# Peer experts: fetches and sums of the 64 gathered tokens spread over the gate groups, shorter tails, and two tensors moved in SBUF

## The chip, the cores and the metric

The program runs on one core of a Trainium2 chip. Its time is the device time of one execution in microseconds (us). The kernel before took 3847.72 us (median of three runs, 3847.21 to 3849.86). The engines are PE (TensorE, with its weight loads shown as PEld), DVE (VectorE), ACT (ScalarE), POOL (GpSimd) and SP (SyncE, here only a queue that starts DMAs).

## The reference

A first block (a two-branch recurrent mixer, then PEER experts) and a second block (attention, MLP, state-space mixer, MLP) act on 512 tokens of width 1024. The change touches mainly the PEER layer. Cut to what matters:

```python
def peer(h, wq, k1, k2, u, v):            # 8 heads, top 16 of 128 x 128 experts per head
    q = (tok @ wq).reshape(-1, 8, 2, 128)
    s1, s2 = q[:, :, 0] @ k1.T, q[:, :, 1] @ k2.T     # 128 scores each, per head
    v1, i1 = top_k(s1, 16); v2, i2 = top_k(s2, 16)
    top_s, top_c = top_k((v1[..., :, None] + v2[..., None, :]).reshape(..., 256), 16)
    expert = i1[top_c // 16] * 128 + i2[top_c % 16]
    gate = softmax(top_s)
    act = gelu(einsum("pd,ped->pe", x, u[expert]))    # 128 experts of a token
    return einsum("pe,ped->pd", gate * act, v[expert])
```

The MLP of the second block is `(relu(h @ w1 + b1) ** 2) @ w2 + b2` with 4096 hidden units.

## The kernel before

Everything is computed with features on the 128 partitions and tokens along the free axis. A float32 product is made of three matmuls of rounded parts (`parts_product`, line 1330): high times high, high times low, low times high. So a weight tile of 128 x 1024 costs 24 matmuls. Its high part is written by ACT (`high`), its low part (raw minus high) by POOL in the first part of the PEER layer (line 1595), by DVE elsewhere.

**Two ways for two groups of tokens.** 448 of the 512 tokens are computed densely: all 16,384 experts' activations for all of them (128 tiles of `u`, the `up(n)` of the code, each 24 matmuls of 448 columns), then a dense matrix of gates, then 128 tiles of `v`. The other 64 tokens (FEW) are computed from gathered rows: two experts' rows for the 64 tokens fill 128 partitions, so 64 calls (CALLS) fetch all rows of `u`, and 64 calls all rows of `v`. `fetch_up` and `fetch_down` are these indirect DMAs, issued by POOL; `few_dots` multiplies a fetched row of `u` with the token and sums it, `few_add` adds a fetched row of `v`, weighted, to a sum in PSUM (line 1953, DVE).

**The gates.** For the dense tokens a gate matrix per token is the product of two one-hot matrices. DVE writes them for eight tokens at a time (`one_hot`: line 2011 one instruction, line 2015 eight), PE multiplies (`gate`, line 1700, 16 records), ACT copies the result from PSUM to the tensor `slab` (line 1806). There are four quarters of the tokens (`TT`), each with 14 such groups. When a quarter is complete, ACT starts four DMAs that write the slab (7.3 MB) to HBM (line 1853). The slab is single: ACT's first copy of the next quarter waits for all four.

**The order.** It is written out by hand, the same in the program of each engine. 48 tiles of `u` go with the eight heads, 7 more (AHEAD) follow while DVE finishes the last top-16. Then for each quarter: 14 gate groups, with one tile of `u` behind those groups for which `between(g)` holds (the last group among them), then a *tail* of TAILS tiles without gates, during which the slab goes out. Tile n uses place p = n + 16 in the stream of weight tiles. POOL's loop runs over the places: it writes the low part of place p, and then issues the fetches that belong to that place. All that stands on POOL is served in order. `fetch_down(c)` waits until the sum number c - 4 is done, since its row's buffer is one of four (OWN), and all later low parts wait behind it. `few_add(c)` on DVE waits for its row to land, and the one-hots of the next quarter stand behind the sums.

Before the change the first four fetches of a quarter are issued two places ahead of its tail, the other twelve by twos at the first six places of the tail (all 16 sums stand behind group 13 on DVE). After the last quarter the `v` tiles begin: each needs an activation tile and a gate tile read back from HBM (`load_pair`, SP), multiplied on DVE (`weigh`).

**Places in SBUF.** Tensors are laid out one behind the other. In the first MLP the moving operand `h_parts` begins where the scan's tables begin, and `w_parts` lies behind the tables, 43,584 bytes per partition further. In the second MLP that distance is 32,768 bytes. In the mixer's output stage `merged_hi` lies at the place of `h`, 118,336 bytes ahead of `w_parts`. The tensor `lb` (64 bytes per partition) lay behind `ident`.

## Time and profile before

| | |
|---|---|
| median of 3 runs | 3847.72 us |
| the profiled execution: its own time, and the span from first to last instruction | 3844.51 us, 3842.7 us |
| PE busy | 3597.3 us, 94% of the span |
| DVE, ACT, POOL busy | 63%, 42%, 33% |
| mean granted TensorE clock | 0.972 |
| the gate section, first gate to first `v` tile | 1446.49 to 1974.32 us: 527.83 us |

PE is the engine to look at. Its idle stretches and the slices in which its clock is granted at half are what a change can win; what the other engines do matters where PE waits for them. In the section below a timeline row has start, duration, engine and line, operation, output<-inputs, shape, number of instructions, and in brackets the idle time before it and what ended it. Ends of matmuls are modelled, so neighbours overlap by some 0.2 us.

### The profile page before, as it was taken

The numbers are of one execution on the slowest core, as the hardware profiler recorded it, in microseconds if no ns is written. First come the engines' busy times: TensorE is split into PE (matmuls) and PEld (weight loads), VectorE is DVE, ScalarE is ACT, GpSimd is POOL, SyncE is SP. The second block draws the span as 40 slices with busy tenths as digits, with TensorE's granted clock in tenths as the row PEclk, the third lists the DMA queues.
The fourth block names the chain that finished last, engine by engine and source line by source line (L and its number), as shares of the span: only waits on it lengthen the run. The fifth ranks groups of instructions, "written<-read, shape, count | busy, mean of one in ns | idle before, by whom it ended". The sixth has DMA issues, their size and how long they took to land. (4 is left out here: it accounts for less than half of the span.)

```text
span 3842.7 us, 47185 instructions
## 1 busy us (share of the span) xinstructions
PE 3597.3 (94%) x18068; PEld 3100.8 (81%) x18068; DVE 2428.3 (63%) x3743; ACT 1622.2 (42%) x2246; POOL 1248.9 (33%) x774
## 2 busy tenths in 40 slices
PE   7999989979999999888999999998999998799998
PEld 6888767768788888878889999996778887677886
DVE  6655534445379988656758878876565475856354
ACT  5555454445242234334434444445542224434222
POOL 1222122137047665354354444441020004402002
PEclk9999989989999999999999999999999999999999
DMA  5111021046247665576498889881123322132331
GB/s 183 55 50 50 17 63 50 23 138 204 103 138 235 222 232 205 204 269 244 154 364 282 285 282 284 285 260 58 42 77 105 98 90 72 29 100 82 99 95 64
DMA packets 245132, 566.26 MB, mean 147 GB/s; under 512 B 91648, under 2 KB 133904, under 8 KB 242736
## 3 DMA queue, kind: packets, MB, share of 16 engines
q1 hardware_dynamic: 203968, 396.31, 31.7%
q0 software_dynamic: 37440, 135.32, 10.5%
q10 hardware_dynamic: 3504, 31.65, 2.1%
q8 instruction: 144, 2.36, 0.2%
q14 instruction: 76, 0.62, 0.1%
HBM read 497.36 MB, written 60.82 MB: 145 GB/s over the span
## 5 line engine op out<-in xcount | busy, mean ns | idle before, releaser
L1330 PE MATMUL peer_banks<-peer_h_parts,peer_w_parts 128*128 128x448 f32 (+1 forms) x3456 | 741.6, 374 | 47.2 <-POOL peer_w_parts L1595 41.4
L1330 PEld LDWEIGHTS peer_banks<-peer_h_parts,peer_w_parts 128*128 128x128 f32 x3456 | 654.0, 191 | 117.4 <-POOL peer_w_parts L1595 51.1
L1330 PE MATMUL peer_banks<-peer_act_parts,peer_w_parts 128*128 128x448 f32 x3072 | 624.3, 365 | 0.0
L1330 PEld LDWEIGHTS peer_banks<-peer_act_parts,peer_w_parts 128*128 128x128 f32 x3072 | 576.3, 188 | 45.4
L1595 POOL TENSOR_TENSOR peer_w_parts<-slots,peer_w_parts 128x1024 fp32r<-128x1024 f32 x142 | 351.5, 2476 | 348.6 <-ACT peer_w_parts L1777 347.0
L1330 PE MATMUL ffn_ps<-h_parts,ffn_w_parts 128*128 128x512 f32 x1920 | 447.5, 395 | 18.0 <-DVE h_parts L2650 11.2
L1330 PEld LDWEIGHTS ffn_ps<-h_parts,ffn_w_parts 128*128 128x128 f32 x1920 | 362.9, 189 | 101.1 <-DVE ffn_w_parts L2488 15.8
L1330 PE MATMUL ffn_ps<-ffn_hidden,ffn_w_parts 128*128 128x512 f32 x1920 | 438.2, 390 | 1.5 <-DVE ffn_hidden L2557 1.5
L1777 ACT ACTIVATE peer_w_parts<-slots 128x1024 fp32r<-128x1024 f32 x272 | 287.1, 1055 | 322.6 <-PE peer_banks L1330 318.6
L1330 PEld LDWEIGHTS ffn_ps<-ffn_hidden,ffn_w_parts 128*128 128x128 f32 x1920 | 360.3, 188 | 77.8 <-issue 3.1
L175 POOL TENSOR_TENSOR peer_slab<-peer_slab 128x1024 f32<-128x1024 f32 x96 | 237.0, 2469 | 258.7 <-ACT peer_slab L182 258.3
L2334 ACT ACTIVATE ffn_w_parts<-slots 128x1024 fp32r<-128x1024 f32 x160 | 168.5, 1056 | 313.1 <-PE ffn_ps L1330 305.5
L2488 DVE TENSOR_TENSOR ffn_w_parts<-slots,ffn_w_parts 128x1024 fp32r<-128x1024 f32 x160 | 197.8, 1240 | 144.2 <-ACT ffn_w_parts L2334 143.8
L2038 DVE TENSOR_TENSOR peer_slab<-peer_slab 128x448 f32<-128x448 f32 x128 | 281.0, 2195 | 7.7 <-DMA peer_slab<-peer_gates 7.7
L1330 PE MATMUL hgrn_proj_ps<-h_parts,hgrn_w_parts 128*128 128x512 f32 x960 | 269.4, 413 | 8.7 <-DVE hgrn_w_parts L986 8.2
L1791 ACT ACTIVATE h<-peer_banks 128x448 f32<-128x448 f32 x128 | 69.7, 544 | 470.0 <-PE peer_banks L1330 434.7
L2048 DVE TENSOR_TENSOR peer_w_parts<-slots,peer_w_parts 128x1024 fp32r<-128x1024 f32 x128 | 157.8, 1233 | 118.5 <-ACT peer_w_parts L1777 118.4
L496 POOL TENSOR_TENSOR hgrn_w_parts<-x,hgrn_w_parts 128x1024 fp32r<-128x1024 f32 x38 | 96.2, 2531 | 342.9 <-ACT hgrn_w_parts L707 342.9
L2301 POOL TENSOR_TENSOR ffn_total<-x 128x512 f32<-128x512 f32 x4 | 5.5, 1379 | 613.9 <-DVE x L2504 613.9
L1330 PEld LDWEIGHTS hgrn_proj_ps<-h_parts,hgrn_w_parts 128*128 128x128 f32 x960 | 168.3, 190 | 39.5 <-DVE hgrn_w_parts L986 8.2
L1330 PE MATMUL gla_proj_ps<-h_parts,gla_w_parts 128*128 128x512 f32 (+1 forms) x600 | 175.7, 432 | 19.8 <-DVE gla_w_parts L1000 14.6
L1953 DVE SCALAR_TENSOR_TENSOR peer_banks<-peer_few_rows,peer_few_w,peer_banks 128x1024 f32<-128x1024 f32 x63 | 81.2, 1288 | 145.8 <-DMA peer_few_rows<-in_peer_v,peer_few_idx 141.3
(579 smaller groups left out, 5773.4 us busy)
## 6 DMA issues: line engine op xcount, KB each, us to landing
slots<-in_peer_u SPq DMA_DIRECT2D x128, 512.0 KB
slots<-in_peer_v SPq DMA_DIRECT2D x128, 512.0 KB
slots<-in_mlp_w SPq DMA_DIRECT2D x128, 512.0 KB, 3.5
peer_slab<-in_w_mod POOLq DMA_DIRECT2D x96, 512.0 KB, 4.5
peer_acts<-h SPq DMA_DIRECT2D x128, 224.0 KB
peer_gates<-peer_slab ACTq DMA_DIRECT2D x16, 1792.0 KB, 14.7
peer_slab<-peer_acts SPq DMA_DIRECT2D x128, 224.0 KB, 5.0
peer_slab<-peer_gates SPq DMA_DIRECT2D x128, 224.0 KB, 5.3
```

The lines of the kernel that those rows point to most:

```text
L175: ins = V_.tensor_tensor(self.prod[:, u, :], self.ring[:, slot, :], self.rows[:, u, :], ALU.mult)
L496: nc.gpsimd.tensor_tensor(wp[:, m % 2, 1, :], ring[m % R], wp[:, m % 2, 0, :].bitcast(F32), ALU.subtract).then_inc(w_lo, 1)
L1330: last = nc.tensor.matmul(out, w(a, k), x(b, k), start=start and k == ks[0] and n == 0, stop=stop and k == ks[-1] and n == 2)
L1595: nc.gpsimd.tensor_tensor(wp[:, p % 2, 1, :], ring.raw[:, p % R, :], wp[:, p % 2, 0, :].bitcast(F32), ALU.subtract).then_inc(w_lo, 1)
L1777: A(wp[:, p % 2, 0, :], ring.raw[:, p % R, :], ACT.Copy).then_inc(w_hi, 1)
L1791: A(stage[:, n % 4, :], a_ps[:, n % 2 * T:n % 2 * T + DENSE], ACT.Gelu).then_inc(gelu_done, 1)
L1953: V.scalar_tensor_tensor(out=few_ps, in0=few_slot(CALLS + c), scalar=w, in1=few_ps, op0=ALU.mult, op1=ALU.add).then_inc(few_added, 1)
L2038: V.tensor_tensor(wact[:, n % 2, :], act_in_sb[:, n % 4, :], gate_in_sb[:, n % 4].rearrange("p b t -> p (b t)"), ALU.mult).then_inc(weight ...
L2048: V.tensor_tensor(wp[:, p % 2, 1, :], ring.raw[:, p % R, :], wp[:, p % 2, 0, :].bitcast(F32), ALU.subtract).then_inc(v_lo, 1)
L2301: st.then(G.tensor_tensor(total[:], K.x[:, 0, :], K.x[:, 1, :], ALU.add))
L2334: A(wp[:, m % 4, 0, :], raw[:, m % R, :], ACT.Copy).then_inc(w_hi, 1)
L2488: V.tensor_tensor(wp[:, m % 4, 1, :], raw[:, m % R, :], wp[:, m % 4, 0, :].bitcast(F32), ALU.subtract).then_inc(w_lo, 1)
```

## The change

In the gate section: eight tiles of `u` move from the tails into the gate groups (a tile now stands behind every group except number 5 and 12), and the tails become 6, 6, 6 and 7 tiles. The sums of fetched `v` rows no longer all stand behind group 13: 3 of the first quarter and 11 of each later quarter follow a group's one-hot each, the tails keep 8, 8, 8 and 4. The fetches get places of their own, each two places behind the place at which the sum that frees its buffer is expected. The last eight fetches of `u` rows are issued by twos at four places, where they were issued by fours at two; their products and the weights stand earlier among the groups. Number and kind of all instructions stay the same.

In SBUF: `lb` moves ahead of `h`, so `h` and all that lies up to `ident`, and `merged_hi` with it, move up by 64 bytes. In the first MLP and the scan behind it a gap of 112 numbers (448 bytes) stands ahead of `w_parts`.

```diff
-        TAILS = (8, 8, 8, 9)
+        TAILS = (6, 6, 6, 7)
         def between(g):
-            return g % 7 in (0, 1, 3, 4, 6)
+            return g % 7 != 5
+        ADD_AFTER = [(11, 12, 13)] + [tuple(range(2, 13))] * 3
+        TAIL_ADDS = (8, 8, 8, 4)
+        def fetch_places():
+            gate_tiles = sum(between(g) for g in range(groups))
+            added = []
+            for tt in range(TT):
+                first = QU + AHEAD + sum(TAILS[:tt]) + tt * gate_tiles
+                added += [first + sum(between(x) for x in range(g)) for g in ADD_AFTER[tt]]
+                added += [first + gate_tiles + m * TAILS[tt] // TAIL_ADDS[tt] for m in range(TAIL_ADDS[tt])]
+            return [78 + c if c < OWN else min(max(82, added[c - OWN] + 2), FRONT - 1) for c in range(CALLS)]
+        places = fetch_places()
...
-                if p == 70:
-                    for c in range(7 * 8, 7 * 8 + OWN):
-                        fetch_up(c)
-                if p == 75:
-                    for c in range(7 * 8 + OWN, CALLS):
-                        fetch_up(c)
+                if p in (69, 70, 73, 74):
+                    c = 7 * 8 + 2 * (69, 70, 73, 74).index(p)
+                    fetch_up(c)
+                    fetch_up(c + 1)
...
-                    if p == tail - 2:
-                        for c in range(16 * tt, 16 * tt + OWN):
-                            fetch_down(c)
-                    if 1 <= p - tail < 7:
-                        c = 16 * tt + OWN + 2 * (p - tail - 1)
+                for c in range(CALLS):
+                    if places[c] == p:
                         fetch_down(c)
-                        fetch_down(c + 1)
...
-                    if tt == 0 and g == 9:
+                    if tt == 0 and g == 7:
                         act.wait_ge(few_dotted, CALLS)
...
-                    if tt == 0 and g == 3:
+                    if tt == 0 and g == 1:
                         few_dots(range(7 * 8, 7 * 8 + OWN))
-                    if tt == 0 and g == 8:
+                    if tt == 0 and g == 6:
                         few_dots(range(7 * 8 + OWN, CALLS))
-                    if tt == 0 and g == 11:
+                    if tt == 0 and g == 10:
                         few_weights()
-                few_add(range(16 * tt, 16 * tt + 16))
+                    if g in ADD_AFTER[tt]:
+                        few_add((c,))
+                        c += 1
+                few_add(range(c, c + TAIL_ADDS[tt]))
+                c += TAIL_ADDS[tt]
...
             keep(alias, "x_alias", [P, KT, T])
+            keep(alias, "lb_alias", [P, 16])
             merged_hi = keep(alias, "merged_hi", [P, KT, T], F32R)
         K.x = keep(ctx, "x", [P, KT, T])
+        K.lb = keep(ctx, "lb", [P, 16])
         K.h = keep(ctx, "h", [P, KT, T])
...
-        K.lb = keep(ctx, "lb", [P, 16])
...
             S = ssm_table_memory(nc, tables)
+            keep(tables, "parts_gap", [P, 112])
             ffn(nc, K, d, 0, hp, S=S)
```

POOL before, from the last fetches of the first quarter's tail to the middle of the second's. L1595 is the low part of a weight tile, L1590 a fetch of `v` rows:

```order
L1595 TENSOR_TENSOR peer_w_parts<-slots,peer_w_parts 128x1024 x10
L1590 DMA peer_few_rows<-in_peer_v,peer_few_idx 128x1024 x4
L1595 TENSOR_TENSOR peer_w_parts<-slots,peer_w_parts 128x1024 x3
L1590 DMA peer_few_rows<-in_peer_v,peer_few_idx 128x1024 x2
L1595 TENSOR_TENSOR peer_w_parts<-slots,peer_w_parts 128x1024
L1590 DMA peer_few_rows<-in_peer_v,peer_few_idx 128x1024 x2
L1595 TENSOR_TENSOR peer_w_parts<-slots,peer_w_parts 128x1024
```

POOL after, the second quarter's last gate groups and the first places of its tail (low parts are L1610, fetches L1605):

```order
L1605 DMA peer_few_rows<-in_peer_v,peer_few_idx 128x1024
L1610 TENSOR_TENSOR peer_w_parts<-slots,peer_w_parts 128x1024
L1605 DMA peer_few_rows<-in_peer_v,peer_few_idx 128x1024
L1610 TENSOR_TENSOR peer_w_parts<-slots,peer_w_parts 128x1024
L1605 DMA peer_few_rows<-in_peer_v,peer_few_idx 128x1024
L1610 TENSOR_TENSOR peer_w_parts<-slots,peer_w_parts 128x1024
L1605 DMA peer_few_rows<-in_peer_v,peer_few_idx 128x1024 x2
L1610 TENSOR_TENSOR peer_w_parts<-slots,peer_w_parts 128x1024
L1605 DMA peer_few_rows<-in_peer_v,peer_few_idx 128x1024
```

Ten low parts in a row with no fetch between them are gone; a fetch stands behind nearly every low part, and two together only where two sums are expected at one place.

DVE before, the end of the second quarter (L2011 and L2015 are a group's one-hots, L1953 the sums):

```order
L2011 TENSOR_TENSOR h<-peer_iota,peer_selt 128x1024
L2015 TENSOR_SCALAR peer_cols<-peer_iota,peer_selt 128x128 x8
L2011 TENSOR_TENSOR h<-peer_iota,peer_selt 128x1024
L2015 TENSOR_SCALAR peer_cols<-peer_iota,peer_selt 128x128 x8
L1953 SCALAR_TENSOR_TENSOR peer_banks<-peer_few_rows,peer_few_w,peer_banks 128x1024 x16
L2011 TENSOR_TENSOR h<-peer_iota,peer_selt 128x1024
```

DVE after, the same place (one-hots L2018 and L2022, sums L1960):

```order
L1960 SCALAR_TENSOR_TENSOR peer_banks<-peer_few_rows,peer_few_w,peer_banks 128x1024
L2018 TENSOR_TENSOR h<-peer_iota,peer_selt 128x1024
L2022 TENSOR_SCALAR peer_cols<-peer_iota,peer_selt 128x128 x8
L1960 SCALAR_TENSOR_TENSOR peer_banks<-peer_few_rows,peer_few_w,peer_banks 128x1024
L2018 TENSOR_TENSOR h<-peer_iota,peer_selt 128x1024
L2022 TENSOR_SCALAR peer_cols<-peer_iota,peer_selt 128x128 x8
L1960 SCALAR_TENSOR_TENSOR peer_banks<-peer_few_rows,peer_few_w,peer_banks 128x1024 x8
L2018 TENSOR_TENSOR h<-peer_iota,peer_selt 128x1024
```

Eight of the sixteen sums are left behind the last group; the others stand one behind each group's one-hots.

## Rows read from the trace of the kernel before

**Rows 1.** Stretches: window, us, busy of PE, PEld, DVE, ACT, POOL; clock, DMA, GB/s

```profile
1446.49:1519.96 73.47, 69.56 (x441) 65.57 (x441) 70.46 (x137) 39.30 (x32) 34.58 (x19) 1.00 0.49 160
1519.96:1580.32 60.36, 46.80 (x220) 42.55 (x218) 24.10 (x24) 15.79 (x20) 33.50 (x22) 0.91 0.90 339
1580.32:1650.34 70.02, 70.02 (x441) 66.91 (x441) 61.27 (x119) 38.99 (x31) 26.25 (x13) 0.98 0.38 128
1650.34:1710.46 60.12, 46.46 (x219) 42.25 (x218) 24.14 (x25) 15.79 (x20) 33.44 (x22) 0.91 0.90 340
1710.46:1781.86 71.40, 71.40 (x441) 68.12 (x441) 61.30 (x119) 38.89 (x31) 26.26 (x13) 0.96 0.38 125
1781.86:1844.32 62.46, 46.70 (x220) 42.47 (x218) 23.63 (x25) 15.80 (x20) 33.47 (x22) 0.88 0.88 328
1844.32:1915.39 71.07, 71.07 (x440) 67.83 (x441) 61.28 (x119) 38.93 (x31) 26.25 (x13) 0.96 0.36 125
1915.39:1974.32 58.93, 51.30 (x244) 46.32 (x242) 22.58 (x21) 16.97 (x22) 33.30 (x25) 0.94 0.97 367
```

**Rows 2.** Timeline of PE, second quarter's tail and the third's first groups

```profile
1650.34 24.56 PE L1330 MATMUL peer_banks<-peer_h_parts,peer_w_parts 128*128 128x448 f32 x120
1684.17 21.90 PE L1330 MATMUL peer_banks<-peer_h_parts,peer_w_parts 128*128 128x448 f32 x96 [9.27 <-POOL peer_w_parts L1595]
1710.46 3.75 PE L1700 MATMUL peer_banks<-peer_cols,h 128*128 128x128 f32 x16 [4.39 <-issue]
1713.87 6.18 PE L1330 MATMUL peer_banks<-peer_h_parts,peer_w_parts 128*128 128x448 f32 x24
```

**Rows 3.** Timeline of POOL, first quarter's tail

```profile
1529.38 0.95 POOL L1590 DMA_INDIRECT peer_few_rows<-in_peer_v,peer_few_idx  x1
...
1544.64 0.96 POOL L1590 DMA_INDIRECT peer_few_rows<-in_peer_v,peer_few_idx  x1 [5.83 <-DVE peer_banks L1953]
...
1551.28 2.35 POOL L1595 TENSOR_TENSOR peer_w_parts<-slots,peer_w_parts 128x1024 fp32r<-128x1024 f32 x1
```

**Rows 4.** Timeline of DVE, first quarter's tail and the second's first group

```profile
1543.08 1.29 DVE L1953 SCALAR_TENSOR_TENSOR peer_banks<-peer_few_rows,peer_few_w,peer_banks 128x1024 f32<-128x1024 f32 x1 [20.53 <-DMA peer_few_rows<-in_peer_v,peer_few_idx]
1548.76 1.29 DVE L1953 SCALAR_TENSOR_TENSOR peer_banks<-peer_few_rows,peer_few_w,peer_banks 128x1024 f32<-128x1024 f32 x1 [4.39 <-DMA peer_few_rows<-in_peer_v,peer_few_idx]
...
1555.53 1.29 DVE L1953 SCALAR_TENSOR_TENSOR peer_banks<-peer_few_rows,peer_few_w,peer_banks 128x1024 f32<-128x1024 f32 x1 [1.15 <-DMA peer_few_rows<-in_peer_v,peer_few_idx]
1557.47 1.29 DVE L1953 SCALAR_TENSOR_TENSOR peer_banks<-peer_few_rows,peer_few_w,peer_banks 128x1024 f32<-128x1024 f32 x1 [0.65 <-DMA peer_few_rows<-in_peer_v,peer_few_idx]
...
1574.08 2.07 DVE L2011 TENSOR_TENSOR h<-peer_iota,peer_selt 128x1024 f32<-128x1024 f32 x1
1576.07 4.15 DVE L2015 TENSOR_SCALAR peer_cols<-peer_iota,peer_selt 128x128 f32<-128x128 f32 x8
1580.14 1.21 DVE L2011 TENSOR_TENSOR h<-peer_iota,peer_selt 128x1024 f32<-128x1024 f32 x1
1581.28 2.13 DVE L2015 TENSOR_SCALAR peer_cols<-peer_iota,peer_selt 128x128 f32<-128x128 f32 x8
```

**Rows 5.** DMA queues from 1519 to 1549: packets, MB, share; q10 carries the slab

```profile
q10 hardware_dynamic: 576, 7.34, 61.4%
```

**Rows 6.** DMA issues of the page: KB each, median us from issue to landing

```profile
peer_slab<-peer_gates SPq DMA_DIRECT2D x128, 224.0 KB, 5.3
```

**Rows 7.** Timelines of DVE and POOL, products of rows beside a low part

```profile
1461.58 1.22 DVE L1943 SCALAR_TENSOR_TENSOR peer_few_rows<-peer_few_rows,peer_banks 128x1024 f32<-128x1024 f32 x1
...
1461.62 2.39 POOL L1595 TENSOR_TENSOR peer_w_parts<-slots,peer_w_parts 128x1024 fp32r<-128x1024 f32 x1 [4.24 <-ACT peer_w_parts L1777]
```

**Rows 8.** Stretches, L1330 on PE alone: mixer output, first MLP, second MLP

```profile
1001.00:1045.00 44.00, 44.00 (x190) 1.00 0.18 63
2840.00:2910.00 70.00, 70.00 (x301) 1.00 0.38 122
3480.00:3550.00 70.00, 70.00 (x310) 1.00 0.32 98
```

More of the change, by code:

```diff
@@ L1509, in peer @@
         AHEAD = 7
-        TAILS = (8, 8, 8, 9)
+        TAILS = (6, 6, 6, 7)
         def between(g):
-            return g % 7 in (0, 1, 3, 4, 6)
+            return g % 7 != 5
         assert EARLY + AHEAD + sum(TAILS) + TT * sum(between(g) for g in range(groups)) == U_TILES
+        ADD_AFTER = [(11, 12, 13)] + [tuple(range(2, 13))] * 3
+        TAIL_ADDS = (8, 8, 8, 4)
+        assert sum(map(len, ADD_AFTER)) + sum(TAIL_ADDS) == CALLS
+        def fetch_places():
[7 more added lines that the diff above has]
+        places = fetch_places()
         @block.sync
@@ L1602, in _ @@
                     fetch_up(8 * h + 2 * (at - 2) + 1)
-                if p == 70:
-                    for c in range(7 * 8, 7 * 8 + OWN):
-                        fetch_up(c)
-                if p == 75:
-                    for c in range(7 * 8 + OWN, CALLS):
-                        fetch_up(c)
+                if p in (69, 70, 73, 74):
+                    c = 7 * 8 + 2 * (69, 70, 73, 74).index(p)
+                    fetch_up(c)
+                    fetch_up(c + 1)
                 if p == 76:
                     spread_gates()
-                for tt in range(TT):
-                    tail = 2 * PEER_H + EARLY + AHEAD + sum(TAILS[:tt]) + (tt + 1) * sum(between(g) for g in range(groups))
-                    if p == tail - 2:
-                        for c in range(16 * tt, 16 * tt + OWN):
-                            fetch_down(c)
-                    if 1 <= p - tail < 7:
-                        c = 16 * tt + OWN + 2 * (p - tail - 1)
+                for c in range(CALLS):
+                    if places[c] == p:
                         fetch_down(c)
-                        fetch_down(c + 1)
             g.wait_ge(slab_out[2], 16 * TT)
@@ L2016, in one_hot @@
                 last.then_inc(cols_done, 1)
+            c = 0
             for tt in range(TT):
```

## The prediction

> **What bounds the kernel now.** I read the stretches first, then PE's timeline, then those of POOL and DVE where PE waits. PE is busy 94% of the span, so a gain must come from PE's idle time, its clock, or the length of a matmul. The gate section has eight stretches, a phase of 14 gate groups and a tail for each quarter [rows 1]. A tile costs (24.56 - 0.24) / 5 = 4.86 us [rows 2]. The third phase takes 71.40 us with 9 tiles (43.8) and 2.9 us of half clock (a gate 3.75 us instead of 1.95, a tile 6.18 instead of 5.10) [rows 1, 2], so a gate group costs (71.40 - 43.8 - 2.9) / 14 = 1.77 us. Then PE needs 73 x 4.86 + 56 x 1.77 = 454 us for the section and takes 527.8: 73.5 us are lost, 16.6, 16.3, 18.7 and 10.3 in the tails (9, 9, 9, 10 tiles are due in them), 4.9, 1.4, 2.8 and 2.5 in the phases.
>
> The tail's loss has two waits. Five tiles run, then PE waits 9.27 us for a low part of POOL; four more run, then it waits 4.39 us for the next quarter's one-hots [rows 2]. The clock falls to its lower level (1.2 of 2.4 GHz) after each: four tiles take 21.90 us instead of 19.7, and the gates behind are slow too; the granted mean of a tail is 0.88 to 0.94 [rows 1]. Why POOL is late: its low parts stand behind fetches, and a fetch stands behind a sum whose row has not landed. I count from the start of the tile behind the last gate (1519.96 in the first quarter, where the row of the first tail begins). A fetch issued at +9.4 is summed at +23.1, the next at +28.8, since the slab's 7.34 MB hold 61.4% of the DMA engines meanwhile [rows 3 to 5]. POOL waits for these two sums and writes the low part at +31.3 [rows 3]; PE wanted it at +24.4. The last sum ends at +54.2 and the one-hots of the next group take until +60.3 [rows 4].
>
> **The change part by part.**
>
> *Tiles.* Eight tiles go from tails to phases: no PE work is added. A phase now needs 11 x 4.86 + 14 x 1.77 = 78.3 us, a tail of 7 tiles 34.0, the last 38.9.
>
> *Sums in the phases.* 36 of the 64 sums leave the tails. In the second phase DVE is busy 61.27 us of which 2.6 are sums, so 58.7 for 13 groups of one-hots [rows 1]. Unhindered a group takes 1.21 + 2.13, less overlap 3.2 [rows 4]; the remaining 17 us are low parts of POOL that hold it up, 9 at 1.9 us each (2.07 and 4.15 instead of 1.21 and 2.13) [rows 4]. With two more low parts and eleven sums at 1.38 DVE needs 58.7 + 3.8 + 15.2 = 77.7 us up to the last gate, PE 76.5. So DVE ends 1.2 us late; I take 1 us per phase. The sums could absorb some low parts: a product of a row runs 1.22 us right beside POOL's 2.39 us subtraction [rows 7], so the bound below is 0. Above: every low part holds DVE for its whole 2.4 us, 41.6 + 11 x 2.4 + 15.2 = 83.2, or 6.7 per phase.
>
> The Trainium skill bears on the same question (SBUF — State Buffer, "SBUF: two separate sides"): DVE and GpSimd share a pair of ports, exclusive for a whole instruction, and DVE takes it with two SBUF inputs or in a two-port mode. The sum reads one operand from PSUM, so by that rule it is not held up, which makes the bound of 83.2 the less likely; the trace's 1.22 us agrees.
>
> *Fetches in the phases.* Each waits for a sum that stands two places earlier, so it is issued without a wait. Its row is needed four sums later, some 13 us behind the issue at the least. The rows show 7.2 us from issue to sum behind the slab (issued just ahead of 1551.28, summed 1557.47) and 13.7 us beside it [rows 3, 4]; in a phase the DMA engines are busy 0.36 to 0.38 instead of 0.90 [rows 1], so I take the lower end and no wait. POOL is busy 26 us of 70 [rows 1], and eleven fetches of 0.95 fit.
>
> *Tails.* Now one row is fetched at +0.8, ahead of the slab, and the one of +9.4 is alone. Second and third quarter: sums end at 24.4 (fetched +9.4), 30.1, 32.5 and 34.4 (the next in the queue, as now), and the last one's fetch waits for the sum at 24.4, as the fifth does now, so that it lands for a sum at +35.5 to +36.8 [rows 4]. POOL passes that place at +26.1 and has the next low part due only then: no wait of PE for POOL. The one-hots end between 3.3 and 6.2 us behind the last sum [rows 4], at about +41.3. PE is through at +34.0: it waits 7.3 us in place of 9.27 and 4.39, and I add 2.5 us for the clock (2.9 behind the second tail). First quarter: it has one sum fewer done ahead, so POOL waits for the sum at +24.4 one tile earlier: the low part ends at +28.1 instead of +23.8, PE waits 3.9 and then 0.6 us. Its last row is fetched at +30.4 and summed at +37.5 to +38.8 [rows 4], one-hots about +43.5: lost 9.5, and 2.5 for the clock. Last quarter: four sums, all fetched early, the last summed by +24.4; no gate follows. The shorter tail takes cover away in two places. The slab is out by about +29, when the rows beside it land [rows 4]; ACT's first copy of the next quarter waits for that, and comes at +34 at the earliest: nothing. The `v` tiles read a gate tile back (5.3 us) [rows 6] and need some 3 us of DVE and ACT on it: 29 + 5.3 + 3 = 37.3, PE is through at 38.9. I leave 0.3 us; if each of these takes twice as long it is 8.
>
> | us lost | now | then |
> |---|---|---|
> | phases | 11.6 | 4 x 1.0 + 3 x 2.5 (clock) |
> | tails | 61.9 | 9.5 + 7.3 + 7.3 + 0.3 |
> | sum | 73.5 | 35.9 |
>
> Gain 37.6 us. The fetches, products and weights of the last head's `u` rows change places in front of and in the first phase; DVE and POOL do the same work for them. At nothing, since PE's tiles cover it; it costs at most what the first phase loses now, 4.9 us, once more, and may win 2 before the first gate.
>
> *Places in SBUF.* This trace has one thing that the instruction lists don't explain: the same product takes 70 / 301 = 232.6 ns in the first MLP and 70 / 310 = 225.8 in the second [rows 8]. What differs is the distance from moving operand to weights: 43,584 bytes, 64 over a multiple of 128, against 32,768, a multiple. The mixer's output with `merged_hi` is slow too (44 / 190 = 231.6 ns), its distance 118,336 is 64 over as well. The change makes them 44,032 and 118,272, both multiples of 128. 960 matmuls (the up halves 2 x 384 and the scan's input 192) at 6.8 ns less missing records, I take 6.4: 6.1 us; 192 in the mixer at 6: 1.2 us. Both stretches are full PE time, so all of it counts: 7.3 us. Bounds 0 and 8.
>
> The Trainium skill speaks against this part (TensorE: Matmul & The Clock Gate, "Step-by-step: what each phase is for"): PE has two independent read ports, and "Loading the next tile's weights doesn't steal SBUF read bandwidth from the running matmul." By it the distance is of no account. The trace's two rates for one product disagree, so I go by the trace.
>
> Sum: 37.6 + 7.3 = 44.9 us. From the profiled execution's 3844.51 that gives 3799.6; the runs' median lies 3.2 us above it, so 3847.7 - 44.9 = 3802.8. I say 3803.
>
> **The rivals.**
>
> *A, DVE becomes the bound of the phases.* At 83.2 us instead of 77.5 it costs 5.7 more in each: + 23, 3826 us. For it: it needs 77.7 against 76.5 already. Against: rows 7. 12%.
>
> *B, the rows are hardly held up.* If the row of +9.4, now alone beside the slab, comes as quickly as behind it (7.2 us), sums end near +26 and the one-hots at +32: no wait in the tails. Then only the phases' 4 us stay lost: 73.5 - 4 + 7.3 = 76.8 us, 3771. Against: the slab's queue holds the engines, not the other row [rows 5]. With half of the tails' 31.9 us it is 3787. 13%.
>
> *C, the other side: POOL's queue closes a ring.* In the phases a fetch that meets its sum undone holds the low part behind it, that the tile, that the next gate. In a tail two such fetches cost 9.27 us, 4.6 each; 33 fetches at 4.6 are 152 us: 3953. It decides from 44.9 / 33 = 1.4 us per fetch. For it: DVE starts each phase with no lead. Against: two places are some 11 us of distance. 4%.
>
> *D, the distances change nothing,* or other operands fall out of step by 64 bytes: 3803 + 7.3 = 3810. For it: one cause inferred from three rates. 11%.
>
> **How the numbers follow.** Forecast 60%. Faster by over 0.2% (7.7 us, about what three runs can tell) holds for the forecast, B, D and nearly all of A: 0.93. Within 0.2%: a mixture of A with longer tails, 0.03. Slower: C, 0.04. The range reaches from two thirds of B (3781) to A (3826).
>
> **What would show it.** Right: PE's stretches before the tiles of the second and third tail without a wait for POOL, one wait of 5 to 9 us before their next gates, ended by DVE's one-hots; no row wait of DVE within the phases; a phase of 79 to 82 us; 310 matmuls in 70 us of the first MLP. Wrong: waits of PE on one-hots inside a phase (A), no wait at the tails' ends (B), idle of POOL on a sum inside a phase (C), 301 matmuls as before (D). Above 3826 or below 3781 my account of the tails is wrong.

## The result and the profile after

The changed kernel takes 3817.43 us (median of four runs, 3815.25 to 3822.50) against 3848.79 us of the kernel before (four runs): ratio 0.9923, 95% interval 0.9911 to 0.9936. So it is 0.8% faster, 31 us, where I had forecast 45. The profiled execution took 3815.25 us with a span of 3813.4 us, 29.3 us less than before.

The eight stretches of the gate section, columns as in [rows 1]:

```profile
1446.65:1526.26 79.61, 78.91 (x489) 74.46 (x489) 75.90 (x138) 43.45 (x38) 41.36 (x21) 1.00 0.50 162
1526.26:1571.67 45.41, 36.12 (x171) 32.75 (x170) 14.81 (x17) 12.80 (x16) 27.78 (x19) 0.93 0.97 392
1571.67:1657.54 85.87, 82.35 (x488) 78.17 (x489) 81.04 (x130) 42.78 (x35) 38.68 (x21) 0.96 0.51 172
1657.54:1698.66 41.12, 34.43 (x171) 31.49 (x170) 13.03 (x16) 12.71 (x15) 25.48 (x16) 0.96 0.94 376
1698.66:1784.11 85.45, 81.93 (x488) 77.87 (x489) 81.25 (x130) 42.73 (x35) 38.68 (x21) 0.96 0.53 182
1784.11:1825.81 41.70, 34.96 (x172) 31.48 (x170) 13.04 (x16) 12.66 (x15) 25.87 (x16) 0.95 0.94 377
1825.81:1910.55 84.74, 81.58 (x489) 77.33 (x489) 80.19 (x130) 42.65 (x35) 38.98 (x21) 0.96 0.51 172
1910.55:1949.99 39.44, 39.26 (x196) 36.04 (x195) 7.66 (x9) 13.64 (x17) 17.47 (x11) 1.00 0.96 369
```

The section takes 503.3 us instead of 527.8 [rows 1], 24.5 less. A phase needs 78.3 us of PE and a tail 34.0 (the last 38.9). So the phases lose 1.3, 7.6, 7.2 and 6.4 us, the tails 11.4, 7.1, 7.7 and 0.5: 49 us where 73.5 were lost, and where I had forecast 35.9. Look at DVE in the phases 2 to 4: it is busy 80 to 81 us. I had forecast 77.7.

PE's timeline in the first tail, and at the end of the second phase with the tail behind it (columns as in [rows 2], which they answer):

```profile
1526.26 24.57 PE L1330 MATMUL peer_banks<-peer_h_parts,peer_w_parts 128*128 128x448 f32 x120
1554.94 11.55 PE L1330 MATMUL peer_banks<-peer_h_parts,peer_w_parts 128*128 128x448 f32 x48 [4.12 <-POOL peer_w_parts L1610]
1571.67 3.76 PE L1707 MATMUL peer_banks<-peer_cols,h 128*128 128x128 f32 x16 [5.18 <-issue]
...
1648.76 1.95 PE L1707 MATMUL peer_banks<-peer_cols,h 128*128 128x128 f32 x16
1654.22 3.65 PE L1707 MATMUL peer_banks<-peer_cols,h 128*128 128x128 f32 x16 [3.52 <-issue]
1657.54 34.43 PE L1330 MATMUL peer_banks<-peer_h_parts,peer_w_parts 128*128 128x448 f32 x168
1698.66 3.67 PE L1707 MATMUL peer_banks<-peer_cols,h 128*128 128x128 f32 x16 [6.69 <-issue]
```

In the tail of the second quarter seven tiles run without a wait and one wait of 6.69 us is left ahead of the next gates, as forecast. New is the wait of 3.52 us between the gates of groups 12 and 13, which follow each other without a tile. It comes back as 3.52 and 3.16 us in quarters 3 and 4. Behind two of the three the gates run at half clock (3.65 and 3.55 us instead of 1.95).

What DVE does there, the answer to [rows 4] (`few_add` is now L1960, the one-hots L2018 and L2022). First the end of the phase, then the tail's waits for rows and the next quarter's first group:

```profile
1647.42 1.27 DVE L1960 SCALAR_TENSOR_TENSOR peer_banks<-peer_few_rows,peer_few_w,peer_banks 128x1024 f32<-128x1024 f32 x1
1648.61 1.21 DVE L2018 TENSOR_TENSOR h<-peer_iota,peer_selt 128x1024 f32<-128x1024 f32 x1
1649.74 4.38 DVE L2022 TENSOR_SCALAR peer_cols<-peer_iota,peer_selt 128x128 f32<-128x128 f32 x8
...
1681.11 1.29 DVE L1960 SCALAR_TENSOR_TENSOR peer_banks<-peer_few_rows,peer_few_w,peer_banks 128x1024 f32<-128x1024 f32 x1 [21.96 <-DMA peer_few_rows<-in_peer_v,peer_few_idx]
...
1692.07 1.29 DVE L1960 SCALAR_TENSOR_TENSOR peer_banks<-peer_few_rows,peer_few_w,peer_banks 128x1024 f32<-128x1024 f32 x1 [0.96 <-DMA peer_few_rows<-in_peer_v,peer_few_idx]
1693.27 1.22 DVE L2018 TENSOR_TENSOR h<-peer_iota,peer_selt 128x1024 f32<-128x1024 f32 x1
1694.40 4.16 DVE L2022 TENSOR_SCALAR peer_cols<-peer_iota,peer_selt 128x128 f32<-128x128 f32 x8
```

And POOL's low part of the same moment:

```profile
1650.53 2.40 POOL L1610 TENSOR_TENSOR peer_w_parts<-slots,peer_w_parts 128x1024 fp32r<-128x1024 f32 x1 [3.13 <-ACT peer_w_parts L1784]
```

DVE's rows stand close: a sum, a one-hot instruction, eight more of the second form, the next sum, with no wait. The eight take 4.38 us instead of 2.13 [rows 4], because POOL's low part (1650.53 to 1652.93) lies in them. One such group is 6.69 us (the sum at 1640.73 and the next at 1647.42), as long as a tile and a gate group of PE (6.65 us from one gate to the next, 1642.11 to 1648.76). So DVE has no lead, and two groups without a tile between them find it late.

At the start of the phase DVE stands idle instead. Its two waits of the whole phase, and its busy time from the phase's start to the moment at which gate 13's one-hots are done:

```profile
1575.47 1.23 DVE L2018 TENSOR_TENSOR h<-peer_iota,peer_selt 128x1024 f32<-128x1024 f32 x1 [0.93 <-PE peer_banks L1707]
1582.42 3.29 DVE L2018 TENSOR_TENSOR h<-peer_iota,peer_selt 128x1024 f32<-128x1024 f32 x1 [2.48 <-PE peer_banks L1707]
```

```profile
1571.67:1654.12 82.45, 78.56 (x129) 0.97 0.50 167
```

The one-hots have two buffers, so those of a group wait for the gate two groups back. DVE can't use a pause at the start for the groups at the end. The low part holds up the first one-hot instruction just as well as the eight: 3.29 us instead of 1.21.

The answer to [rows 8], L1330 on PE in the same windows:

```profile
1001.00:1045.00 44.00, 42.59 (x188) 1.00 0.17 60
2840.00:2910.00 70.00, 70.00 (x310) 1.00 0.36 114
3480.00:3550.00 70.00, 70.00 (x311) 1.00 0.32 101
```

The first MLP now has 310 matmuls in 70 us, the mixer's output 42.59 / 188 = 226.5 ns per matmul instead of 231.6. The PEER layer begins at 1057.6 us instead of 1059.6. In this execution the clock came up later behind that start (the layer's first 48 matmuls took 14.09 us; 13.37 before, 12.50 with the moves alone), and the section begins no sooner than before (389.1 us from the layer's start to the first gate; 386.9 before, 385.3 to 389.1 in the kernels below). The span's 29.3 us are thus 24.5 in the section, 6.2 in the first MLP and 2.0 ahead of the PEER layer, less 2.2 between there and the first gate and 1.2 given back elsewhere, which I haven't followed.

### The profile page after: what moved, and what is told of

It is laid out like the page before. It is cut to its first block and busy times, and to the rows that moved or that the text cites. A ratio compares the mean times of both kernels' runs of the same rounds, so it can differ in the third digit from the quotient of the medians.

```text
span 3813.4 us, 47185 instructions
## 1 busy us (share of the span) xinstructions
PE 3588.6 (94%) x18068; PEld 3100.5 (81%) x18068; DVE 2451.7 (64%) x3743; ACT 1624.1 (43%) x2246; POOL 1258.5 (33%) x774
## 5 line engine op out<-in xcount | busy, mean ns | idle before, releaser
L1330 PE MATMUL peer_banks<-peer_h_parts,peer_w_parts 128*128 128x448 f32 (+1 forms) x3456 | 739.7, 373 | 15.1 <-POOL peer_w_parts L1610 9.3
L1330 PEld LDWEIGHTS peer_banks<-peer_h_parts,peer_w_parts 128*128 128x128 f32 x3456 | 650.1, 190 | 84.4 <-POOL peer_w_parts L1610 18.1
L1330 PE MATMUL peer_banks<-peer_act_parts,peer_w_parts 128*128 128x448 f32 x3072 | 624.5, 365 | 0.0
L1330 PEld LDWEIGHTS peer_banks<-peer_act_parts,peer_w_parts 128*128 128x128 f32 x3072 | 576.3, 188 | 45.7 <-issue 0.3
L1610 POOL TENSOR_TENSOR peer_w_parts<-slots,peer_w_parts 128x1024 fp32r<-128x1024 f32 x142 | 352.5, 2482 | 350.2 <-ACT peer_w_parts L1784 348.7
L1330 PE MATMUL ffn_ps<-h_parts,ffn_w_parts 128*128 128x512 f32 x1920 | 441.9, 392 | 18.5 <-DVE h_parts L2662 11.3
L1330 PEld LDWEIGHTS ffn_ps<-h_parts,ffn_w_parts 128*128 128x128 f32 x1920 | 363.5, 190 | 95.5 <-DVE ffn_w_parts L2500 15.9
L1330 PE MATMUL ffn_ps<-ffn_hidden,ffn_w_parts 128*128 128x512 f32 x1920 | 438.1, 390 | 1.5 <-DVE ffn_hidden L2569 1.5
L1330 PEld LDWEIGHTS ffn_ps<-ffn_hidden,ffn_w_parts 128*128 128x128 f32 x1920 | 360.3, 188 | 77.7 <-issue 3.1
L1330 PE MATMUL hgrn_proj_ps<-h_parts,hgrn_w_parts 128*128 128x512 f32 x960 | 269.4, 413 | 8.7 <-DVE hgrn_w_parts L986 8.2
L1330 PEld LDWEIGHTS hgrn_proj_ps<-h_parts,hgrn_w_parts 128*128 128x128 f32 x960 | 168.1, 190 | 39.7 <-DVE hgrn_w_parts L986 8.2
L1330 PE MATMUL gla_proj_ps<-h_parts,gla_w_parts 128*128 128x512 f32 (+1 forms) x600 | 175.8, 432 | 19.9 <-DVE gla_w_parts L1000 14.7
L2022 DVE TENSOR_SCALAR peer_cols<-peer_iota,peer_selt 128x128 f32<-128x128 f32 x448 | 173.0, 461 | 0.0
```

Of the source, the lines that this page charges most:

```text
L1330: last = nc.tensor.matmul(out, w(a, k), x(b, k), start=start and k == ks[0] and n == 0, stop=stop and k == ks[-1] and n == 2)
L1610: nc.gpsimd.tensor_tensor(wp[:, p % 2, 1, :], ring.raw[:, p % R, :], wp[:, p % 2, 0, :].bitcast(F32), ALU.subtract).then_inc(w_lo, 1)
L2022: last = V.tensor_scalar(cols[:, b, t, :], iota[:], selt[:, 1, one], selt[:, 2, one], ALU.is_equal, ALU.mult)
```

## The experiments

The kernel before was timed again beside each set of runs (medians 3846.0, 3847.0 and 3847.3 us; 3840.7 in a single run beside the last), and the ratios are to it. Sections are counted here to the first matmul of a `v` tile, by which the changed kernel's is 503.5 us.

**The order alone** (the changed kernel without the moves in SBUF).

```diff
-            keep(alias, "lb_alias", [P, 16])
-        K.lb = keep(ctx, "lb", [P, 16])      # back behind ident
-            keep(tables, "parts_gap", [P, 112])
```

> The changed kernel with `lb` and `w_parts` where they were before: only the order of tiles, sums and fetches is changed. My theory, that matmuls are slowed when moving operand and weights lie 64 bytes off a multiple of 128 apart: the first MLP takes 6.1 us more and the mixer's output 1.2 to 2 us more than in the changed kernel, 3817.4 + 7.3 = 3824.7 us, 0.6% faster than before, and the first MLP's matmuls are 233 ns apart again instead of 226. Rival D, that the distances change nothing: 3817.4 us. The order alone is then worth 24 us by the first and 31 by the second.

Measured: 3823.42 us, ratio 0.9943 (0.9926 to 0.9960), a section of 504.4 us. **The moves alone** (the kernel before with these three lines):

> The kernel before with the two moves in SBUF alone. My theory: 3848.8 - 7.3 = 3841.5 us, with 226 to 227 ns per matmul in the first MLP and 226.5 in the mixer's output, and a gate section of 527 to 528 us as before. Rival D: 3848.8 us and 233 ns. A second point: in the changed kernel the first tiles of the PEER layer ran with half clock for 3.4 us longer than before. If that comes from the earlier start by the moves, it shows here too, and the gain is 4 to 5 us instead of 7 to 8.

Measured: 3841.80 us, ratio 0.9985 (0.9968 to 1.0002), a section of 529.0 us. I expected 3841.5 us, 7.3 less than the 3848.8 of the first timing. Beside this run the kernel before had 3846.0, so the difference is 4.2, and the interval reaches no change: the times alone don't show this part. The traces do. The first MLP's matmuls as a group (count, busy us, mean ns, idle before), first of the order alone, then of the moves alone:

```profile
L1330 PE MATMUL ffn_ps<-h_parts,ffn_w_parts 128*128 128x512 f32 x960 | 227.2, 398 | 5.5 <-DVE ffn_w_parts L2500 4.2 <-DVE h_parts L2569 1.2
```

```profile
L1330 PE MATMUL ffn_ps<-h_parts,ffn_w_parts 128*128 128x512 f32 x960 | 221.5, 393 | 5.6 <-DVE ffn_w_parts L2488 4.2 <-DVE h_parts L2557 1.4
```

Each kernel has the rate of its layout, whatever its order. In spans the moves are worth 3821.7 - 3813.4 = 8.3 us in the one pair and 3842.7 - 3836.0 = 6.7 in the other, the order 21.0 and 22.6. The theory holds and rival D falls. The later clock at the start of the PEER layer doesn't follow from them: with the moves alone it took 387.7 us to the first gate, and of the other executions below three have it (13.96 to 14.06 us for the first 48 matmuls).

**Which distance counts.** Three gaps of other sizes.

```diff
-            keep(tables, "parts_gap", [P, 112])
+            keep(tables, "parts_gap", [P, 16])      # then 80, then 48
```

> The changed kernel with a gap of 16 numbers instead of 112 ahead of `w_parts`, so the distance from `h_parts` to `w_parts` in the first MLP is 43,648 bytes: 341 x 128, but not a multiple of 256 or more, as 44,032 = 43 x 1024 is. If a multiple of 128 bytes is what counts: 226 to 227 ns per matmul and 3817.4 us as the changed kernel. If it takes a multiple of 256, 512 or 1024: 233 ns and 3817.4 + 6.1 = 3823.5 us.

> The changed kernel with a gap of 80 numbers ahead of `w_parts`: the distance from `h_parts` is 43,904 bytes, 256 over a multiple of 512. With a gap of 16 (128 over a multiple of 512) the first MLP's matmuls took 232 to 233 ns, with 112 (a multiple of 512) 227, with none (64 over) 233. If a multiple of 512 is what counts, this one takes 232 to 233 ns; if a multiple of 256 does, 227. If the slow rate with a gap of 16 was an accident of that run and multiples of 128 are enough, 227 too.

> The changed kernel with a gap of 48 numbers ahead of `w_parts`: the distance from `h_parts` is 43,776 bytes, 256 over a multiple of 512. (With a gap of 80 it was 43,904, which is 384 over, not 256 as written ahead of that run; so that one told only that a multiple of 128 isn't enough.) If multiples of 256 do, the first MLP's matmuls take 227 ns; if it takes a multiple of 512, 232 to 233. The `v` stage, which ran at 206.7 ns in both executions of the gap of 16 and at 202.7 in all other kernels: no theory of mine says which; 202.7 by the count of kernels.

(The distance with the gap of 80 is 43,904 bytes, 384 over a multiple of 512, as the last of these says.)

The gap of 16 measured 3825.08 us, ratio 0.9939 (0.9918 to 0.9959); the other two were single executions, 3817.92 and 3809.26 us. Their first MLP, in this order:

```profile
L1330 PE MATMUL ffn_ps<-h_parts,ffn_w_parts 128*128 128x512 f32 x960 | 226.7, 398 | 5.3 <-DVE ffn_w_parts L2500 4.2 <-DVE h_parts L2569 1.1
```

```profile
L1330 PE MATMUL ffn_ps<-h_parts,ffn_w_parts 128*128 128x512 f32 x960 | 227.3, 398 | 5.3 <-DVE ffn_w_parts L2500 4.2 <-DVE h_parts L2569 1.1
```

```profile
L1330 PE MATMUL ffn_ps<-h_parts,ffn_w_parts 128*128 128x512 f32 x960 | 221.6, 393 | 5.6 <-DVE ffn_w_parts L2500 4.2 <-DVE h_parts L2569 1.4
```

43,648 and 43,904 bytes, both multiples of 128 and 128 over a multiple of 256, are slow; 43,776 (171 x 256) is fast, as 44,032 is. So my rule of 128 was wrong: these distances want a multiple of 256. The gap moves the weights and leaves the moving operand where it was. In the mixer's output it is the other way round, and the rate changed with the distance too (231.6 to 226.5 ns), so it isn't the place of one of the two alone. Why such distances cost time no run shows.

The gap of 16 had a surprise: its whole `v` stage was slow too. From 2000 to 2100 us PE does 486 matmuls there, the changed kernel 495.

> The kernel with the gap of 16 numbers once more. In its first profiled execution not only the first MLP ran at 232 to 233 ns per matmul, but the whole `v` stage at 206.7 instead of 202.7 (12 us longer), where nothing of the layout differs from the changed kernel. If the `v` rate belongs to the execution, it is 202.7 here; if to the kernel, 206.7. The first MLP: 232 to 233 ns again, if it takes a multiple of 512 bytes between the operands; 227 if the slow rate there was part of the same accident.

Measured: 3831.14 us, and again 485 matmuls in that window (206.7 ns from one to the next on average, 202.7 in all other kernels) and a slow first MLP. So the `v` rate went with this kernel twice, though nothing in the layout of that stage differs. But its timed runs spread from 3813 to 3834 us, and the lowest leaves little room for 12 us in that stage. The cause stays open.

**The one-hots ahead of the late sums.** In each tail DVE does two sums, then the one-hots of the next quarter's groups 0 and 1, then the other sums.

```diff
-                    one_hot(tt * groups + g)
+                    if tt == 0 or g >= 2:
+                        one_hot(tt * groups + g)
...
-                few_add(range(c, c + TAIL_ADDS[tt]))
+                few_add(range(c, c + 2))
+                if tt + 1 < TT:
+                    one_hot((tt + 1) * groups)
+                    one_hot((tt + 1) * groups + 1)
+                few_add(range(c + 2, c + TAIL_ADDS[tt]))
```

> The changed kernel with DVE's one-hots of the next quarter's groups 0 and 1 placed ahead of all but the first two sums of a tail (they stood behind all eight). My theory, that a tail's remaining wait of PE is DVE's one-hots queued behind sums that wait for rows beside the slab: the one-hots are done about 10 us before PE wants them, the waits of 5.2, 6.7 and 6.7 us go, and with them most of the half clock behind them (2.5 to 3 us each): 18.6 + 8 = 26.6 us less at the most, 3791 us. Part of it can come back, since the late sums now stand ahead of group 2's one-hots: two groups of lead are 2 x 6.6 = 13 us, and the last sum ends only 2 to 6 us behind PE's tail, so I expect at most 2 us back for each quarter: 3791 to 3797. Rival: PE waits there for ACT's copy, which waits for the slab: then nothing changes, 3817. A third way: POOL's fetches wait longer in the tail because sums are 13 us later, and PE waits for low parts instead: 3805 to 3815.

Measured: 3789.41 us, ratio 0.9863 (0.9841 to 0.9885), a little less than the 3791 to 3797 that I expected; a section of 475.3 us instead of 503.5. PE in the second quarter:

```profile
1643.49 2.02 PE L1707 MATMUL peer_banks<-peer_cols,h 128*128 128x128 f32 x16 [3.52 <-issue]
1645.27 34.30 PE L1330 MATMUL peer_banks<-peer_h_parts,peer_w_parts 128*128 128x448 f32 x168
1679.40 1.95 PE L1707 MATMUL peer_banks<-peer_cols,h 128*128 128x128 f32 x16
```

And DVE: the last of the early one-hots, then the last late sum and eight one-hots of group 2:

```profile
1650.21 2.14 DVE L2022 TENSOR_SCALAR peer_cols<-peer_iota,peer_selt 128x128 f32<-128x128 f32 x8
...
1680.10 1.29 DVE L1960 SCALAR_TENSOR_TENSOR peer_banks<-peer_few_rows,peer_few_w,peer_banks 128x1024 f32<-128x1024 f32 x1 [1.05 <-DMA peer_few_rows<-in_peer_v,peer_few_idx]
1682.53 4.23 DVE L2022 TENSOR_SCALAR peer_cols<-peer_iota,peer_selt 128x128 f32<-128x128 f32 x8
```

Seven tiles in 34.30 us, and the gate follows without a wait at full clock. The third tail is the same, so these two are gone from the loss; the first keeps a wait of 3.43 us for POOL's low part. So what was left in the tail was one-hots standing in the queue behind sums that wait for rows beside the slab. The rival (the slab holds ACT's copy) falls. The wait ahead of gate 13 stays (3.52, 3.16 and 3.16 us, now without half clock behind it), so its cause lies in the phase, not in the tail before.

**POOL's low parts cut short,** to tell why DVE is late in the phase.

```diff
-                nc.gpsimd.tensor_tensor(wp[:, p % 2, 1, :], ring.raw[:, p % R, :], ...
+                w = 16 if p >= 71 else KT * P
+                nc.gpsimd.tensor_tensor(wp[:, p % 2, 1, 0:w], ring.raw[:, p % R, 0:w], ...
```

> The changed kernel with POOL's low parts of the weight tiles from place 71 on cut to 16 columns (the other columns of the low part are left out, so this is not the whole computation); PE, DVE and ACT do all they did. It tells whether DVE is late in a phase because POOL's low part holds its one-hots up (eight tensor_scalar 4.3 us instead of 2.13 beside a low part of 2.42). If so, DVE gains some 2 us per tile, 20 us per phase, and the waits of 3.5, 3.5 and 3.2 us ahead of gate 13 go with the clock behind them (13.6 us); POOL is not late in the first tail either (4.1 us and 3 of clock), and the one-hots at a tail's end come up to 2 us sooner: 20 to 26 us less, 3791 to 3797. Rival, that DVE's own work in a phase is too much and POOL has no part in it: the waits stay, 3810 to 3817.

Measured: 3797.42 us, ratio 0.9856 (0.9829 to 0.9883), a section of 486.1 us. DVE in the third phase, a group:

```profile
1707.83 1.23 DVE L2019 TENSOR_TENSOR h<-peer_iota,peer_selt 128x1024 f32<-128x1024 f32 x1 [2.17 <-PE peer_banks L1708]
1708.98 2.14 DVE L2023 TENSOR_SCALAR peer_cols<-peer_iota,peer_selt 128x128 f32<-128x128 f32 x8
1711.03 1.28 DVE L1961 SCALAR_TENSOR_TENSOR peer_banks<-peer_few_rows,peer_few_w,peer_banks 128x1024 f32<-128x1024 f32 x1
```

And PE at the end of that phase, groups 12 and 13 as one row of 32:

```profile
1760.86 3.73 PE L1708 MATMUL peer_banks<-peer_cols,h 128*128 128x128 f32 x32
```

The eight one-hots take 2.14 us, DVE has 2.2 us to spare in most groups and waits for PE, and the three waits ahead of gate 13 are gone. The same work of DVE is early without the low part and late with it, so the hold-up by POOL is the cause, at some 2.2 us per tile. The median lies 20.0 us below the changed kernel's, the least that I expected: the tails keep their waits for one-hots (5.65, 4.98 and 4.52 us), and behind the last tail PE waits 6.0 us for the read of the gate tiles here.

**A tile between groups 12 and 13.**

```diff
-            return g % 7 != 5
+            return g not in (5, 13)
```

> The changed kernel with a tile of `u` behind group 12 of each quarter as well, so that of the pairs of groups without a tile between them only 5/6 is left; each tail has one tile fewer. In the changed kernel PE waits 3.5, 3.5 and 3.2 us ahead of gate 13 in quarters 2 to 4. My theory, that DVE there runs in step with PE (one group of one-hots per tile and gate, 6.65 us) and has no lead for two groups without a tile: these three waits go, with the half clock behind two of them (1.7 us each), 13.6 us in the phases. But each of the three tails before a gate has one tile (4.86 us) less ahead of the same one-hots, so waits of 5.2, 6.7 and 6.7 us grow by up to 4.9 - 3.4 = 1.5 to 4.9 us each: the wait moves from the phase into the tail, 3810 to 3818 us. Rival, that DVE is behind by its total work in a phase: the wait ahead of gate 13 stays at 2 to 3 us and the tails grow by 4.9: 3830 us.

Measured: 3823.12 us, ratio 0.9928 (0.9902 to 0.9955), a section of 510.6 us, above what I expected. PE at the second quarter's end, then at the fourth's:

```profile
1655.21 1.95 PE L1707 MATMUL peer_banks<-peer_cols,h 128*128 128x128 f32 x16
1656.92 9.97 PE L1330 MATMUL peer_banks<-peer_h_parts,peer_w_parts 128*128 128x448 f32 x48
...
1698.20 3.49 PE L1707 MATMUL peer_banks<-peer_cols,h 128*128 128x128 f32 x16 [10.82 <-issue]
```

```profile
1909.37 35.02 PE L1330 MATMUL peer_banks<-peer_h_parts,peer_w_parts 128*128 128x448 f32 x168
1953.53 0.66 PE L1761 MATMUL peer_banks<-peer_fold,peer_few_rows 128*128 128x64 f32 x2 [9.14 <-DVE peer_w_parts L2060]
```

In the first three quarters it went nearly as said: no wait ahead of gate 13, phases of 85 us as in the changed kernel with one more tile in them, and tail waits of 10.7, 10.8 and 11.3 us instead of 5.2, 6.7 and 6.7 (4.1 to 5.5 more; I had said 1.5 to 4.9). The miss is the last tail, which I left out: with seven tiles it no longer covers the read of the gate tiles, and PE waits 9.1 us.

**The sums back in the tails,** with the new tiles and distances.

```diff
-        ADD_AFTER = [(11, 12, 13)] + [tuple(range(2, 13))] * 3
-        TAIL_ADDS = (8, 8, 8, 4)
+        ADD_AFTER = [(11, 12, 13)] + [()] * 3
+        TAIL_ADDS = (13, 16, 16, 16)
```

> The changed kernel with the sums of quarters 2 to 4 all in the tails again (13, 16, 16, 16 sums), and the fetches at the places that follow from it; tiles, distances and the rest as in the changed kernel. By my account the sums in the phases cost DVE 1.4 us each and take the waits ahead of gate 13 with them, but in a tail they cost as much and wait for rows beside the slab as well: the waits ahead of gate 13 vanish (10 us and 3.4 of clock), and each tail of quarters 1 to 3 ends with DVE's one-hots at about +55 to +60 instead of +41 to +45, with PE through at +34: 3 x 15 to 18 us more. Together 32 to 40 us more than the changed kernel: 3850 to 3857, no faster than before. Rival, that the shorter tails and the fetches' places alone are what won: 3804 to 3817.

Measured: 3861.76 us, ratio 1.0031 (1.0014 to 1.0048), slower than before and than I expected. The second quarter's tail on PE:

```profile
1694.04 12.50 PE L1330 MATMUL peer_banks<-peer_h_parts,peer_w_parts 128*128 128x448 f32 x48 [9.63 <-POOL peer_w_parts L1610]
1717.37 3.75 PE L1707 MATMUL peer_banks<-peer_cols,h 128*128 128x128 f32 x16 [10.83 <-issue]
```

The phases 2 to 4 take 81 us (4.4 less each, groups 12 and 13 close together), the tails 54.7, 58.2, 57.3 and 58.7 (61 us more in all). Again I had left out the last tail, 19 of these. Shorter tails alone win nothing: they lose what the sums in them cost.

**Together, with one sum less at a phase's end.** The order of the one-hots as above, and:

```diff
-        ADD_AFTER = [(11, 12, 13)] + [tuple(range(2, 13))] * 3
-        TAIL_ADDS = (8, 8, 8, 4)
+        ADD_AFTER = [(10, 11, 12, 13)] + [tuple(range(2, 12))] * 3
+        TAIL_ADDS = (7, 9, 9, 5)
```

> The one-hots of the next quarter's groups 0 and 1 ahead of a tail's late sums, as in that experiment (its gate section took 475.3 us, 3778.5 us of span, median 3789.4), and besides a sum less at the end of each of the phases 2 to 4 (none behind group 12; it goes to the tail) and one sum more in the first phase, behind group 10. My theory is that DVE's load in a phase sets the waits ahead of gate 13: a sum of 1.29 us less makes them 1.9 to 2.2 us instead of 3.5, 3.2 and 3.2 (3.9 us together), and POOL, which in the first tail stood one sum behind the other quarters, doesn't hold PE up there (3.4 us of wait and 3 of half clock): a gate section of 465 to 467 us, 3779 to 3781. Rival, that the ninth sum in a tail makes DVE late for group 2 instead: what the phases gain comes back as a wait ahead of gate 2 of 1 to 3 us, 472 to 476 us and 3786 to 3790.

Measured: 3785.12 us, ratio 0.9835 (0.9810 to 0.9861), a section of 471.4 us, 4 less than without it and between the two theories. PE around the second tail:

```profile
1637.57 3.77 PE L1707 MATMUL peer_banks<-peer_cols,h 128*128 128x128 f32 x32
1641.10 29.64 PE L1330 MATMUL peer_banks<-peer_h_parts,peer_w_parts 128*128 128x448 f32 x144
1673.94 6.74 PE L1330 MATMUL peer_banks<-peer_h_parts,peer_w_parts 128*128 128x448 f32 x24 [3.20 <-POOL peer_w_parts L1610]
```

The waits ahead of gate 13 vanish altogether (phases of 78.5 to 78.8 us, PE's bare need), more than the 1.3 us of one sum. DVE's last one-hots of that phase and POOL's low part show why:

```profile
1637.09 2.14 DVE L2022 TENSOR_SCALAR peer_cols<-peer_iota,peer_selt 128x128 f32<-128x128 f32 x8
```

```profile
1639.34 2.38 POOL L1610 TENSOR_TENSOR peer_w_parts<-slots,peer_w_parts 128x1024 fp32r<-128x1024 f32 x1 [3.13 <-ACT peer_w_parts L1784]
```

A sum earlier, the eight are done just before the low part begins and take 2.14 us instead of 4.38, so the sum of 1.2 us took a hold-up of 2.2 with it. But with nine sums in a tail a fetch stands before a sum and holds up a low part: PE waits 3.2 and 1.5 us in the second and third tail, where it had no such wait with eight. Some of the gain comes back, then, but in POOL's queue, not ahead of gate 2 as the rival had it. The first tail keeps its wait for POOL as well (3.0 us), which I had expected to go. Its time and that of the kernel without it (3789.4) overlap in their intervals; both are faster than the changed kernel.

## Why the prediction was right in kind and its gain too large

| term | forecast | measured |
|---|---|---|
| places in SBUF | 7.3 | 6.2 in the first MLP, 2.0 ahead of the PEER layer |
| tails, us lost | 24.4; 9.5, 7.3, 7.3, 0.3 | 26.7; 11.4, 7.1, 7.7, 0.5 |
| phases, us lost with the clock | 11.5 | 22.5 |
| gain in the section | 37.6 | 24.5 |

**Sums in the phases** is the step that failed, at "So DVE ends 1.2 us late". I had added up DVE's work, 77.7 us up to the last gate, and set it against PE's 76.5 as if DVE worked without a pause from the phase's start. The work was sized nearly right, 78.56 us. But gate 13's one-hots were done 82.45 us behind the start (1571.67 to 1654.12), since DVE was idle for 3.9 of them, 3.4 in the two waits for PE at groups 2 and 3. PE, itself 2.5 us later by half clock behind the tail, wanted them at +79.0 and waited 3.5 us, not 1.

Within the work two terms were off and nearly made up for each other. A sum adds 1.19 us (1647.42 to 1648.61), not 1.38. A low part costs DVE 2.2 us (eleven cost 23.9), not 1.9. I had divided the 17 us by nine low parts, but in the phase before eight of them held one-hots up, in full though DVE had pauses, and the ninth lay beside sums. The first of the eight:

```profile
1590.13 2.42 POOL L1595 TENSOR_TENSOR peer_w_parts<-slots,peer_w_parts 128x1024 fp32r<-128x1024 f32 x1 [10.25 <-ACT peer_w_parts L1777]
```

```profile
1590.35 3.28 DVE L2011 TENSOR_TENSOR h<-peer_iota,peer_selt 128x1024 f32<-128x1024 f32 x1 [3.36 <-PE peer_banks L1700]
```

"The sums could absorb some low parts" did not come about: in the changed kernel all eleven low parts of a phase fall into one-hots, as at 1649.74 to 1654.12, none beside a sum. So rival A, to which I gave 12%, came half true: phases 2 to 4 take 85.3 us instead of 81.8, held by DVE at gate 13. The median of 3817 lies between my 3803 and A's 3826.

The price of a late DVE is paid at one place, the pair of groups without a tile, where PE wants two groups 1.8 us apart: 3.5, 3.5 and 3.2 us and, twice, 1.7 of clock, where my sum had 1 us each and no clock.

**Tails.** Right: the one-hots at the second tail's end let the gate go at +41.1 us (forecast +41.3) behind one wait of 6.7 (7.3), the first tail's wait for POOL is 4.12 us (3.9), and the row of +9.4 (here +9.9) was summed at +23.6. Too small in the first tail, where the gate came at +45.4 instead of +43.5: the last sum began at +38.3 (forecast +37.5 to +38.8), and the one-hots behind it ran beside a low part (4.60 us). The "0.6" of the prediction is a slip: one-hots at +43.5 and PE through at 34.0 + 3.9 = 37.9 make 5.6 us, which with the 3.9 give the 9.5 of its sum. Measured are 4.12 and 5.18 us, and between them two tiles at half clock take 11.55 us instead of 9.97. Rival B falls by the same rows: the lone row still took its time beside the slab. That the 6.7 us were sums ahead of one-hots is shown by the kernel that turns them round.

**The last tail.** The 0.3 us were right by a hair: the eight tiles cover the read of the gate tiles here (0.5 us lost). With seven they do not (9.1 us), nor do eight in the kernel with the short low parts (6.0), so the read itself takes longer in some kernels, and I haven't followed why.

**Fetches in the phases.** Right: POOL never waits for a sum there, and no row is late for its sum; the ring of rival C doesn't close.

**Places in SBUF.** The size was right, and the traces of eleven other kernels or executions go with the distance. The rule as I put it, a multiple of 128, was too weak. Of the 2.0 us ahead of the PEER layer, 192 matmuls at 5.1 ns make 1.0; the layer's start varies from 1055.0 to 1057.6 us among the kernels with the moves, so the rest isn't shown.

The Trainium skill (SBUF — State Buffer, "SBUF: two separate sides") has DVE and GpSimd share a port pair, one whole instruction at a time. I used it for the sum, where the trace agrees. A sum in the first tail and the low part beside it:

```profile
1558.01 1.29 DVE L1960 SCALAR_TENSOR_TENSOR peer_banks<-peer_few_rows,peer_few_w,peer_banks 128x1024 f32<-128x1024 f32 x1 [1.18 <-DMA peer_few_rows<-in_peer_v,peer_few_idx]
```

```profile
1558.08 2.40 POOL L1610 TENSOR_TENSOR peer_w_parts<-slots,peer_w_parts 128x1024 fp32r<-128x1024 f32 x1
```

The one-hots are the other side of it, and there the rows show the hold-up nearly in full: 2.1 to 2.3 us of the low part's 2.4.

## What to carry to other kernels

When work is moved onto an engine that has had pauses, don't compare its added work with the stretch: ask which pauses it can use. With two buffers DVE could not work ahead in the pauses at a phase's start, and it was late at the end. Where an engine runs in step with another, look for the one place at which two steps follow without the usual work between them, since there its missing lead is paid. And ahead of work that others wait for, no wait for a DMA should stand in the queue: turning the one-hots of two groups and six sums round was worth more (28 us of the section) than all else that the change did to the order (21 to 25).

## What the runs showed of the hardware that I had not expected

- A 128x512 matmul whose weights are loaded each time comes every 226.7 ns on average when moving operand and weights lie a multiple of 256 bytes apart (32,768, 43,776, 44,032 and 118,272), and every 232 to 233 when they lie 64 or 128 bytes off one (43,584, 43,648, 43,904, 118,336). Other distances were not tried.
- Eight tensor_scalar instructions with one tensor input each (2.13 us) take 4.2 to 4.7 us beside a GpSimd subtraction of 2.4 us, and the 128x1024 tensor_tensor 3.3 instead of 1.21; the sum that reads PSUM takes 1.29 us beside it as without it.
- One kernel's `v` stage (448 columns) ran at 206.7 ns per matmul in both profiled executions, all others at 202.7, with the same addresses in that stage. This is not explained.
